# Choice of experts moved out of the routing stage and into the output projection, in a 4096-token hybrid layer

## What is computed

```python
u = rms(x) * g1;  q, k, v, x_lru, g_lru = split(u @ w_in)
out_A = stick_breaking_attention(q, k, v)          # 8 heads of 64, causal
out_B = rglru(conv4(x_lru)) * gelu(g_lru)          # 8 blocks of 64
h = x + concat(rms(out_A), rms(out_B)) @ w_out
u2 = rms(h) * g2
group = argmax(u2 @ w_group + b_group)             # 1 of 4 groups
top2 = top_2(u2 @ w_fine + b_fine, inside group)   # 2 of the group's 8 experts
h = h + sum over top2 of weight * (silu(u2 @ w_gate[e]) * (u2 @ w_up[e])) @ w_down[e]
y = rms(h) * g_final
```

## Time and profile before

| | us |
|---|---|
| median of 3 runs | 4645.36 (4645.25 to 4648.19) |
| the profiled execution, its own time | 4648.48 |
| its span in the trace | 4646.4 |
| stages ahead of `mix` | 0 to 2519 |
| `mix` | 2519 to 3051 |
| `route` | 3051 to 3159 |
| `experts` | 3159 to 4646.4 |

### The profile page before, as it was taken

One profiled execution on the slowest core, in us unless ns is written; L12 is line 12 of the kernel. 1 busy time (PEld: TensorE's weight loads), 2 busy tenths in 40 slices (PEclk: granted clock), 3 DMA queues, 4 the chain that ended last, 5 costly groups with the idle time before them and its releaser, 6 DMA issues. The chain is left out here.

```text
span 4646.4 us, 85418 instructions
## 1 busy us (share of the span) xinstructions
PE 4282.4 (92%) x28496; PEld 3206.5 (69%) x28497; DVE 2892.6 (62%) x3384; ACT 2518.9 (54%) x3914; POOL 605.7 (13%) x771
## 2 busy tenths in 40 slices
PE   6999979996999998999996999938999999999998
PEld 5878767774555555555554888837888878888886
DVE  3222245665998998999995333375656555555665
ACT  3222224444787887888885323213656555555665
POOL 0000002221000000000000000021223232222322
PEclk9999989998999999999998999969999999999999
DMA  4222231111201102001002333334656555554663
GB/s 136 90 100 104 85 120 54 54 52 41 91 29 52 34 29 63 22 29 63 4 9 79 143 138 130 123 127 147 247 204 245 199 207 197 192 205 169 247 246 141
DMA packets 279572, 539.95 MB, mean 116 GB/s; under 512 B 38321, under 2 KB 103857, under 8 KB 279345
## 3 DMA queue, kind: packets, MB, share of 16 engines
q1 hardware_dynamic: 228512, 410.49, 25.0%
q0 software_dynamic: 46224, 118.03, 7.3%
q10 hardware_dynamic: 4608, 8.39, 0.5%
HBM read 410.97 MB, written 176.16 MB: 126 GB/s over the span
## 5 line engine op out<-in xcount | busy, mean ns | idle before, releaser
L945 DVE TENSOR_TENSOR_SCAN att_R<-att_stay,att_R 128x512 f32<-128x512 f32 x896 | 1058.9, 1261 | 25.8 <-ACT att_stay L885 23.5
L895 ACT ACTIVATE att_RT<-att_rt 128x512 f32<-128x512 f32 (+3 forms) x1152 | 585.8, 562 | 234.0 <-PE att_rt L836 204.5
L836 PEld LDWEIGHTS att_rt<-ident,att_R 64*128 64x128 f32 x8448 | 319.8, 139 | 372.0 <-issue 368.3
L885 ACT ACTIVATE att_stay<-att_z 128x1024 f32<-128x1024 f32 (+2 forms) x576 | 555.5, 965 | 25.2 <-PE att_z L823 23.7
L849 PE MATMUL att_out<-att_RT,att_dv 128*64 128x512 f32 (+3 forms) x2304 | 521.9, 574 | 0.0
L836 PE MATMUL att_rt<-ident,att_R 64*128 64x64 f32 x8448 | 384.0, 227 | 98.5 <-ACT att_RT L895 53.4
L1257 DVE TENSOR_TENSOR ew_lo<-ew_raw,ew_hi 128x1024 fp32r<-128x1024 f32 x372 | 430.1, 1218 | 13.6 <-ACT ew_hi L1250 13.6
L1250 ACT ACTIVATE ew_hi<-ew_raw 128x1024 fp32r<-128x1024 f32 x384 | 373.8, 1047 | 97.3 <-PE ex_down L1680 97.3
L243 PE MATMUL qkv_out<-qkv_u_hi,qkv_w_hi 128*128 128x512 f32 x768 | 308.8, 402 | 18.2 <-DVE qkv_u_lo L234 18.2
L243 PE MATMUL qkv_out<-qkv_u_hi,qkv_w_lo 128*128 128x512 f32 x768 | 303.4, 395 | 0.0
L243 PE MATMUL qkv_out<-qkv_u_lo,qkv_w_hi 128*128 128x512 f32 x768 | 300.9, 392 | 0.0
(11 more groups left out here) (262 smaller groups left out, 8430.6 us busy)
## 6 DMA issues: line engine op xcount, KB each, us to landing
ew_raw<-in_w_e_gate SPq DMA_DIRECT2D x32, 2048.0 KB
ew_raw<-in_w_e_up SPq DMA_DIRECT2D x32, 2048.0 KB
ew_raw<-in_w_e_down SPq DMA_DIRECT2D x32, 2048.0 KB
qkv_x<-in_x SPq DMA_DIRECT2D x32, 512.0 KB, 5.0
lru_x<-in_x SPq DMA_DIRECT2D x32, 512.0 KB, 4.9
mix_raw<-s_mix_t SPq DMA_DIRECT2D x32, 512.0 KB, 4.1
mix_x<-in_x SPq DMA_DIRECT2D x32, 512.0 KB, 4.8
s_h<-mix_h SPq DMA_DIRECT2D x32, 512.0 KB, 3.5
```

The costliest lines, as they stand in the source:

```text
L836: last = nc.tensor.transpose(rt[half][:, h, qt, :], R[lanes, n % 3, h, qt, s * P:(s + 1) * P], k.ident[lanes, lanes])
L885: done = nc.scalar.activation(pair(stay[:, step % 4, :]), pair(z[step % 2][:]), ACT.Sigmoid, scale=-scale)
L895: nc.scalar.activation(RT[:, :, s, first:, half, :], rt[half][:, :, first:, :], ACT.Copy).then_inc(rt_copied[half], 1)
L945: nc.vector.tensor_tensor_scan(R[:, n % 3, h, s, 0:width][:, ::-1], src[:, ::-1], src[:, ::-1], initial, ALU.mult, ALU.bypass).then_inc(sc ...
```

## The change

The selection is made by a new function `select` in `mix`: 21 linked DVE instructions for 4 tiles (512 tokens), once a group, behind `u2` of the first tile of the next group, and for the last group after the last logits. It writes `g_dist`, `dist`, `first` and `both` for its group into buffers that live on. In `route` the one-hots are rebuilt from `first`; PE's matmuls no longer wait for DVE; the totals are made in expert order and scanned straight from PSUM; the integer steps are done for both choices together; and in each turn the product with `weight` is 8 activations of 128x98 on ACT (semaphore `coded` from DVE to ACT, `hot_ready` from ACT to PE). ACT makes the high parts of the gate matrix ahead of the turns and of the two others behind them. The low parts of expert 0 move from POOL in `route` to DVE in `experts`, around `x_low(dve, 0)`, and with them the load of expert 1 moves to `experts`. A buffer `junk` in `mix` is dropped (the squares go to `u2`, which is overwritten after).

```diff
+            def select(dve, G):
+
+                count = [0]
+                V = nc.vector
+
+                def link(instruction):
+                    count[0] += 1
+                    instruction.then_inc(select_step, 1)
+                    dve.wait_ge(select_step, G * SELECT_STEPS + count[0] + 1)
...
+                dve.wait_ge(logits_ready, G * TT + TT + 1)
+                link(V.tensor_reduce(s_max[:], logit[:, :, 0:NGRP], AX.X, ALU.max))
+                link(V.tensor_tensor(g_dist, logit[:, :, 0:NGRP], spread(s_max[:], NGRP), ALU.subtract))
+                link(V.tensor_scalar(s_pen[:], g_dist, 0.0, None, ALU.is_equal))
+                link(V.scalar_tensor_tensor(s_cand[:], s_pen[:], -2.0 * NE, along(NGRP), ALU.mult, ALU.add))
+                link(V.tensor_reduce(s_first[:], s_cand[:], AX.X, ALU.min))
+                link(V.tensor_tensor(s_pen[:], s_cand[:], spread(s_first[:], NGRP), ALU.is_equal))
+                link(V.tensor_scalar(s_pen[:], s_pen[:], -MASKED, MASKED, ALU.mult, ALU.add))
+                link(V.tensor_tensor(grouped(s_fine[:]), grouped(logit[:, :, NGRP:]),
+                                     s_pen[:].unsqueeze(3).to_broadcast([P, TT, NGRP, EPG]), ALU.add))
+                for c in range(TOPK):
+                    found = s_hot if c == 0 else s_eq
+                    first = k.first[:, c, bass.ds(G * TT, TT)]
+                    link(V.tensor_reduce(s_top[c][:], s_fine[:], AX.X, ALU.max))
+                    link(V.tensor_tensor(s_eq[:], s_fine[:], spread(s_top[c][:], NE), ALU.is_equal))
+                    link(V.scalar_tensor_tensor(s_eq[:], s_eq[:], -2.0 * NE, along(NE), ALU.mult, ALU.add))
+                    link(V.tensor_reduce(first, s_eq[:], AX.X, ALU.min))
+                    link(V.tensor_tensor(found[:], s_eq[:], spread(first, NE), ALU.is_equal))
+                    if c == 0:
+                        link(V.scalar_tensor_tensor(s_fine[:], s_hot[:], 3 * MASKED, s_fine[:], ALU.mult, ALU.add))
+                link(V.tensor_tensor(k.both[:, bass.ds(G * TT * NE, TT * NE)].rearrange("p (t e) -> p t e", e=NE),
+                                     s_hot[:], s_eq[:], ALU.add))
...
             def _(pool):
+                nc.gpsimd.iota(iota_i[:], pattern=[[1, P]], base=0, channel_multiplier=0).then_inc(iota_made, 1)
                 groups(pool, pool_group)
...
                     nc.vector.scalar_tensor_tensor(u2[:, t, :], h[:, t, :], rinv2[:], g_norm2[:],
                                                    ALU.mult, ALU.mult).then_inc(u2_ready, 1)
+                    if t == 0 and not first:
+                        select(dve, G - 1)
...
                 dve.wait_ge(params, 48)
+                dve.wait_ge(iota_made, 1)
+                nc.vector.tensor_copy(k.iota[:], iota_i[:]).then_inc(select_step, 1)
                 dve_low(dve, 0, 0)
                 weights.low(dve)
                 groups(dve, dve_group)
-                dve_logits(dve, NT - 1)
+                dve_logits(dve, NT - 1, RING - 1)
+                dve.wait_ge(select_step, (NG - 1) * SELECT_STEPS + 1)
+                select(dve, NG - 1)
...
         @block.gpsimd
         def _(pool):
-            nc.gpsimd.iota(iota_i[:], pattern=[[1, P]], base=0, channel_multiplier=0)
             nc.gpsimd.iota(token_i[:], pattern=[[P, NT]], base=0, channel_multiplier=1)
             nc.gpsimd.memset(ones_e[:], 1.0)
             nc.gpsimd.memset(seg[:], 1.0).then_inc(iota_ready, 1)
             pool.wait_ge(iota_ready, 1)
             nc.gpsimd.memset(seg[:, :, 0:1], 0.0).then_inc(iota_ready, 1)
-            for m in range(MATRICES):
-                weights.low(pool, m, 0)
 
         @block.sync
         def _(sp):
-            for e in range(2):
-                weights.load(sp, e)
+            weights.load(sp, 0)
 
         @block.scalar
         def _(act):
-            act.wait_ge(g_dist_ready, 1)
-            nc.scalar.activation(g_exp[:], g_dist[:], ACT.Exp).then_inc(g_exp_ready, 1)
-            act.wait_ge(dist_ready, 1)
-            nc.scalar.activation(ratio[:], dist[:], ACT.Exp).then_inc(ratio_ready, 1)
-            for m in range(MATRICES):
+            nc.scalar.activation(g_exp[:].rearrange("p t n -> p (t n)"), k.g_dist[:], ACT.Exp).then_inc(g_exp_ready, 1)
+            nc.scalar.activation(ratio[:], k.dist[:], ACT.Exp).then_inc(ratio_ready, 1)
+            weights.high(act, 0, 0)
+            for turn in range(TOPK * NT // BT):
+                c, t = divmod(turn * BT, NT)
+                act.wait_ge(coded, turn + 1)
+                for i in range(BT):
+                    row = row_facts[turn % 2][:, i, 1, :]
+                    last = nc.scalar.activation(row, row, ACT.Copy, scale=weight[:, c, t + i:t + i + 1])
+                last.then_inc(hot_ready, 1)
+            for m in range(1, MATRICES):
                 weights.high(act, m, 0)
...
         @block.tensor
         def _(pe):
-            pe.wait_ge(both_ready, 1)
+            by_expert = k.both[:].rearrange("p (t e) -> p e t", e=NE)
             for i in range(2):
-                nc.tensor.matmul(prefix[i][:], k.before[:], both[:, i * GT:(i + 1) * GT], start=True, stop=True)
+                last = nc.tensor.matmul(total[:, i * GT:(i + 1) * GT], k.ones_bf[:], by_expert[:, i * NE // 2:(i + 1) * NE // 2, :],
+                                        start=True, stop=True)
+            last.then_inc(counted, 1)
             for i in range(2):
-                last = nc.tensor.matmul(total[i][:], k.ones_bf[:], both[:, i * GT:(i + 1) * GT], start=True, stop=True)
+                last = nc.tensor.matmul(prefix[i][:], k.rest[:], k.both[:, i * GT:(i + 1) * GT], start=True, stop=True)
             last.then_inc(counted, 1)
...
             for c in range(TOPK):
-                link(V.tensor_reduce(top[c][:], fine[c], AX.X, ALU.max))
-                link(V.tensor_tensor(eq[:], fine[c], spread(top[c][:], NE), ALU.is_equal))
-                link(V.scalar_tensor_tensor(cand[:], eq[:], -2.0 * NE, along(NE), ALU.mult, ALU.add))
-                link(V.tensor_reduce(first[c][:], cand[:], AX.X, ALU.min))
-                link(V.tensor_tensor(hot[c], cand[:], spread(first[c][:], NE), ALU.is_equal))
-                if c == 0:
-                    link(V.scalar_tensor_tensor(fine[1], hot[0], 3 * MASKED, fine[0], ALU.mult, ALU.add))
-            link(V.tensor_tensor(both[:].rearrange("p (t e) -> p t e", e=NE), hot[0], hot[1], ALU.add))
-            done(both_ready)
-            link(V.tensor_tensor(dist[:], top[1][:], top[0][:], ALU.subtract))
-            done(dist_ready)
+                link(V.scalar_tensor_tensor(hot[c], along(NE), -2.0 * NE, spread(k.first[:, c, :], NE), ALU.add, ALU.is_equal))
+            link(V.tensor_tensor(later[:], k.first[:, 0, :], k.first[:, 1, :], ALU.is_gt))
+            for c, (sign, base_code) in enumerate(((LATER, VALID), (-LATER, VALID + LATER))):
+                link(V.scalar_tensor_tensor(token_code[:, c, :], later[:], float(sign), token_f[:], ALU.mult, ALU.add))
+                link(V.tensor_scalar(token_code[:, c, :], token_code[:, c, :], float(base_code), None, ALU.add))
...
             dve.wait_ge(counted, 1)
-            for i in range(2):
-                half = NT // 2
-                link(V.tensor_copy(totals[:, :, i * half:(i + 1) * half], total[i][:].rearrange("p (t e) -> p e t", e=NE)))
-            flat = lambda ap: ap[:].rearrange("p e t -> p (e t)")
-            link(V.tensor_tensor_scan(flat(upto), flat(seg), flat(totals), 0.0, ALU.mult, ALU.add))
-            link(V.tensor_tensor(base[:], upto[:], totals[:], ALU.subtract))
+            link(V.tensor_tensor_scan(sums[:, 1, :], seg[:].rearrange("p e t -> p (e t)"), total[:], 0.0, ALU.mult, ALU.add))
...
-            link(V.scalar_tensor_tensor(base[:], start_f[:].unsqueeze(2).to_broadcast([P, NE, NT]), float(P), base[:], ALU.mult, ALU.add))
+            link(V.scalar_tensor_tensor(base[:], start_f[:].unsqueeze(2).to_broadcast([P, NE, NT]), float(P), upto, ALU.mult, ALU.add))
+            dve.wait_ge(counted, 2)
...
             for c in range(TOPK):
                 link(V.tensor_tensor(picked[:], slot_all[:], hot[c], ALU.mult))
-                link(V.tensor_reduce(slot_f[:], picked[:], AX.X, ALU.add))
-                link(V.tensor_copy(slot_i[:], slot_f[:]))
-                link(V.tensor_scalar(lane_i[:], slot_i[:], P - 1, None, ALU.bitwise_and))
-                link(V.tensor_scalar(row_i[:], slot_i[:], 7, None, ALU.logical_shift_right))
-                link(V.tensor_copy(lane_f[:, c, :], lane_i[:]))
-                link(V.tensor_copy(row_f[:, c, :], row_i[:]))
+                link(V.tensor_reduce(slot_f[:, c, :], picked[:], AX.X, ALU.add))
+            link(V.tensor_copy(slot_i[:], slot_f[:]))
+            link(V.tensor_scalar(lane_i[:], slot_i[:], P - 1, None, ALU.bitwise_and))
+            link(V.tensor_scalar(row_i[:], slot_i[:], 7, None, ALU.logical_shift_right))
+            link(V.tensor_copy(lane_f[:], lane_i[:]))
```

(9 more changed lines are left out.)

86 lines of the change are left out of this document (38 added, 48 removed).

## The result

The changed kernel takes 4614.98 us in the median of 4 runs (4610.57 to 4616.88). The kernel before, run beside it on the same chip, takes 4645.98 (4645.25 to 4648.19). The ratio is 0.9931, with a 95% interval of 0.9914 to 0.9948: 31 us less, where 33.5 were forecast. The profiled execution takes 4610.57, with a span of 4608.8.

What follows compares the result with a forecast made beforehand. PE bounds `mix` and `experts`, DVE's linked chain bounds `route`. 38.1 us won up to the turns less 4.6 lost in turns and tail gives 33.5: 4615.0 for the profiled execution, 4611.9 in the median, range 4603 to 4619.

Steps and rivals of the forecast that it cites:

- Up to the turns: In `route`, ahead of the first turn: last `select` and new chain take 24.8 us instead of 62.9, so 38.1 earlier.
- The place of the selection: Selection moved from `route` to `mix`: some 19 us, seven times out of eight hidden; the last group's 5.9 stays exposed.
- POOL's silence: In `route`, ten small DVE instructions no longer wait behind POOL's low parts, 2.1 us extra each: some 21 us.
- the ring of two buffers: In the turns, DVE's turn k+2 waits for PE's turn k: 8.6 us for two turns, 4.3 each, against 4.5 before.
- ACT's burst: In each turn, ACT's 8 activations of 128x98 take 2.2 us, between bounds of 1.35 and 2.3.
- The list: Turns to block's end with tail: full clock 44.3, even turns at half clock 47.7, nearly all slow 49.2, short burst 41.1.
- The 46.0: Turns and tail in `route`: taken midway between 44.3 and 47.7, 4.6 us longer than the 41.4 before.
- The rival with half clock in nearly every turn: In the turns, PE stays at half clock: block's end 49.2, gain 30.3, time 4615; chance 0.20.
- The cheap ring: In the turns, ACT's burst is 1.35 and PE keeps its clock: gain 38.4 to 40.6, 4602 to 4607; chance 0.15.
- The tail: At `route`'s end, ACT's remaining high parts hold the barrier: up to 2.2 us, nothing if it passes a running activation.
- the slack that was read from one tile: In `mix`, `select` takes up to 7.2 us and may last 10.4 before PE stalls; nothing charged.
- hid the low parts: In `experts`, DVE's low parts of expert 0 cost 0, with 3 us to spare at the up matrix.

Runs made afterwards that it cites:

- `again`: The changed kernel itself, unaltered, run and profiled a second time on another chip: 4617.36 us, ratio 0.9933 to the kernel before.
- 3: Changed kernel with `select` taken out of `mix` and put over all 32 tiles at the start of `route`: 4629.83 us, ratio 0.9960.
- 2: Kernel before with only expert 0's low parts moved to DVE in `experts`, and expert 1's load behind them: 4625.03 us, ratio 0.9954.
- 5: Changed kernel with all twelve of ACT's high parts of expert 0 ahead of the turns: 4614.34 us, ratio 0.9930.
- 7: Changed kernel with 18 more unused DVE steps in each `select` inside `mix`, not the last: 4632.54 us, ratio 0.9966.
- 8: Changed kernel with the logits matmuls in `mix` moved ahead by one group of 12 wide matmuls, away from the sums: 4592.91 us, ratio 0.9881.
- 9: Changed kernel with three turn buffers, all high parts ahead of the turns, and wide matmuls between logits and sums: 4577.56 us, ratio 0.9850.

## Why the prediction was right

The terms, against two profiled executions of the changed kernel (us, less than before is negative; before is the profiled execution of the tables above):

| | forecast | after | `again` |
|---|---|---|---|
| last logits to first turn | -38.1 | -37.9 | -37.9 |
| first turn to index copy | +4.6 | +3.3 | +5.7 |
| up to the last logits | 0 | -2.5 | -1.1 |
| index copy to the end | 0 | -0.5 | -0.1 |
| span | -33.5 | -37.6 | -33.4 |

**Up to the turns** the count of instructions was right to 0.2. Its halves are shown apart. The place of the selection is worth 12.7 (3), where 19 less the 5.9 that stay behind the last logits were forecast, 13.1. POOL's silence is worth 23.5 in the stage (2) and 23.3 of that up to the first turn, some 21 for the ten small instructions and the rest in longer ones. The shorter slot chain is what remains of 37.9, 1.9. For the scan's lower bound, 2.3, the prediction shows no row; it took 2.29.

**The turns** went as the ring of two buffers was written down: ACT's burst of 2.24 for 2.2, two turns in 8.6 where the even one kept its clock (8.6 forecast) and in 10.3 where it didn't, PE waiting for ACT, DVE for PE, and a net loss. The list had 44.3 (all later turns at full clock) and 47.7 (even turns cold). Up to the copy 45.8 and 48.1 were measured, and the copy lies 1.0 behind the block's end in the kernel before: 44.8 and 47.1. The second is the case of cold even turns. The first is a mixture, with one of three later even turns slow; the case at full clock throughout came in no trace of this ring. The 46.0 was the middle between two cases and was not worked out. It held because the executions fall on both sides of it: in the five traces with two buffers and the tail (after, `again`, 3, 7, 8) this stretch is longer than before by 3.3, 5.7, 6.3, 5.0 and 4.9, for 4.6.

What lets PE keep the clock is open, and the length of the wait alone doesn't decide it. In the six traces with two buffers and ACT in the ring there are 18 even turns behind the first. After 3.02 of idle time all 11 were slow (4.5 to 4.6), after 2.28 three of four (4.3 to 4.5), but after 2.70 to 2.80 all three were at full clock (2.92).

The rival with half clock in nearly every turn has 4615 as its time, and that is where the median came. The time alone can't tell the two apart; the traces do: odd turns took 2.8 to 3.2 in all of them, not 4.7. The cheap ring did not occur either, since the burst has the size of the upper bound. (By its own gains its time would be 4604.8 to 4607, not from 4602.)

**The tail** is there and is the barrier's (5). It was put at 2.2 behind a last pair at full clock and at 1.0 behind a cold even turn; in both executions the last even turn is slow (4.31 and 4.57), and the tail costs 0.9, the size for that case.

**`mix`** had the slack that was read from one tile: 10.2 by experiment 7 for 10.4. `select` takes 7.3 for 7.2, one step held up by POOL. The -2.5 and -1.1 in the table are not `select`'s. From the first `u2` to the last logits it is -3.1 in after and +1.6 in `again`, which fits 14 and 17 long tiles against 16. The rest, +0.6 and -2.7, lies ahead of the first `u2`, which comes at 2560 to 2566 in the traces of all these kernels.

**`experts`** hid the low parts, with 4 to spare for 3 at the up matrix and 1.3 at the first tile's tokens.

The median came 3.1 above the forecast and the profiled execution 4.4 below it. The step from the execution to the median took over the 3.1 by which the profiled execution of before lies above its median, while the one of after is the fastest of its four. Long tiles (1.55 each) and even turns (1.7 each) are what differs between the traces of the changed kernel; they are of the size of the spread of its nine runs, 8.6 us, but only the profiled ones show which they had.

## What to carry to other kernels

Before a product is moved to a third engine inside a ring, count how many buffers the ring has: with two, the new stage is added to the cycle, and an engine that has become faster gains nothing; here one more buffer, with ScalarE's high parts put ahead of the turns (worth 0.9), turned a loss of 4 to 6 us against the stage without ScalarE (70.0) into a gain of 5 to 6 (64.7 and 63.7). When small instructions on VectorE take ten times their size, look at what GpSimd does at that moment, and move its work first: it was the largest single part, for a few lines. And test a slack read from the trace by padding, since the same experiment shows where the wait appears and how long it is.

## What the hardware showed that was not expected

TensorE's granted clock fell to 0.50 in stretches in which the engine was never idle, behind the logits and the sums, 2.6 us of matmuls with 36 columns and one column. This happened in 14 to 17 of 31 tiles, differently in each execution, and cost 1.55 us a time. With 12 wide matmuls between the two it happened in none (experiments 8 and 9), and `mix` became 22 us shorter. A busy share of 1.00 does not show this; the column of the granted clock in short windows does.
